# Router products in column tiles and modulation chunks spread over the q/k products, in a two-layer diffusion step on one core

## The reference, cut to what matters

```python
def grouped_moe(h, w_router, router_bias, w_gate, w_up, w_down):
    t = h.reshape(-1, D)                                    # 640 tokens, D = 1024
    scores = jax.nn.sigmoid((t @ w_router).astype(f32))     # 16 experts
    biased = scores + router_bias
    # best of 4 groups by the sum of its two best, then the best 2 experts in it
    ...
    gates = ...                                             # normalised scores of the two
    act = silu(t @ w_gate[e]) * (t @ w_up[e]) * gates
    return act @ w_down[e], summed over e

for layer in range(2):
    shift_a, scale_a, gate_a, shift_f, scale_f, gate_f = split(silu(cond) @ w_ada[layer] + b, 6)
    h = modulate(rmsnorm(x, norm_mix[layer]), shift_a, scale_a)
    out = mla(h) if layer == 0 else neighbourhood_attention(qkv(h))
    x = x + gate_a * (out @ w_o)
    h = modulate(rmsnorm(x, norm_ffn[layer]), shift_f, scale_f)
    x = x + gate_f * grouped_moe(h, ...)
```

## Time and profile before

| | |
|---|---|
| median of 3 runs | 1524.39 us (1524.38 to 1531.06) |
| the profiled execution | 1526.28 us, span 1524.5 us |
| PE busy | 1306.5 us, 86% of the span |
| DVE, ACT, POOL busy | 495.0, 357.3, 262.5 us |
| mean granted clock of TensorE | 0.936 of full speed |

### The profile page before, as it was taken

The page is one execution under the profiler, slowest core; times in us unless marked ns, Lnnn a source line. Parts: engine busy times, 40 slices in busy tenths (PEclk is TensorE's granted clock), DMA queues, the critical chain, the costliest instruction groups (busy, mean ns, idle before and its releaser), DMA issues.

```text
span 1524.5 us, 19501 instructions
## 1 busy us (share of the span) xinstructions
PE 1306.5 (86%) x7230; PEld 756.4 (50%) x7230; DVE 495.0 (32%) x1249; ACT 357.3 (23%) x843; POOL 262.5 (17%) x374
## 2 busy tenths in 40 slices
PE   3899899999999678999839989998999968999980
PEld 2565466666555434444324445556774543444430
DVE  2221344444345511112261000005663661111227
ACT  3221344444312101111132000005662210111112
POOL 6112201000100131111050111301110013111104
PEclk9999999999999689999959999999999968999995
DMA  7723112211532648898762464503204144889855
GB/s 271 278 91 110 56 57 78 91 57 57 197 142 84 235 132 331 325 343 338 280 257 75 166 209 166 180 0 98 64 22 157 42 179 145 332 328 351 326 225 206
DMA packets 48616, 269.87 MB, mean 177 GB/s; under 512 B 9709, under 2 KB 16269, under 8 KB 34829
## 3 DMA queue, kind: packets, MB, share of 16 engines
q1 hardware_dynamic: 22588, 192.87, 34.9%
q0 software_dynamic: 18176, 47.65, 8.7%
q10 hardware_dynamic: 7776, 28.32, 4.6%
HBM read 235.49 MB, written 31.74 MB: 175 GB/s over the span
## 4 chain that ended last, share of the span: by engine, by line
PE 65%; DMA 16%; DVE 7%; issue 5%; ACT 3%; POOL 1%; SPq 1%; ACTq 0%; POOLq 0%; DVEq 0%; PEldq 0%
PE PS L735 12%; DMA weights<-in_gu 11%; PE PS L948 9%; PE PS L1068 9%; PE PS L986 8%; PE PS L657 7%; PE PS L1003 5%; PE PS L854 4%; PE PS L669 3%; PE PS L885 2%; DVE big L1464 2%; DMA resid<-in_x 2%; PE PS L813 2%; DMA weights<-in_ada 1%; PE PS L895 1%
## 5 line engine op out<-in xcount | busy, mean ns | idle before, releaser
L986 PE MATMUL PS<-weights,big 128*128 128x512 f32 x544 | 249.2, 612 | 27.7 <-DMA weights<-in_gu 24.2
L986 PEld LDWEIGHTS PS<-weights,big 128*128 128x128 f32 x544 | 103.5, 195 | 152.4 <-issue 152.2
L657 PE MATMUL PS<-const,big 128*128 128x128 f32 (+2 forms) x643 | 99.6, 296 | 72.4 <-ACT big L1171 28.5
L948 PE MATMUL PS<-weights,ht 128*128 128x512 f32 x320 | 144.1, 606 | 1.7 <-DVE ht L1464 1.6
L657 PEld LDWEIGHTS PS<-const,big 128*128 128x128 f32 (+2 forms) x643 | 82.8, 151 | 121.0 <-issue 68.1
L1068 PE MATMUL PS<-ht,weights 128*128 128x128 f32 (+1 forms) x512 | 140.2, 434 | 1.6 <-PE PS L669 1.0
L735 PE MATMUL PS<-weights,ht 128*128 128x336 f32 (+1 forms) x320 | 122.0, 540 | 6.4 <-DVE ht L1555 2.4
L1003 PE MATMUL PS<-weights,big 128*128 128x512 f32 x272 | 124.8, 602 | 1.8 <-DVE big L1867 1.8
L1068 PEld LDWEIGHTS PS<-ht,weights 128*128 128x128 f32 x512 | 77.8, 191 | 64.4 <-issue 64.4
L1464 DVE TENSOR_TENSOR big<-big,PS 128x256 f32<-128x256 f32 x34 | 14.3, 421 | 267.0 <-ACT big L1370 257.6
L948 PEld LDWEIGHTS PS<-weights,ht 128*128 128x128 f32 x320 | 60.6, 194 | 73.1 <-issue 73.1
(11 more groups left out here) (204 smaller groups left out, 1611.8 us busy)
## 6 DMA issues: line engine op xcount, KB each, us to landing
weights<-in_gu SPq DMA_DIRECT2D x34, 2048.0 KB, 11.5
weights<-in_ada SPq DMA_DIRECT2D x24, 2048.0 KB, 8.3
weights<-in_down SPq DMA_DIRECT2D x34, 1024.0 KB, 5.8
yrows<-big ACTq DMA_DIRECT2D x34, 512.0 KB, 10.4
weights<-in_qkv SPq DMA_DIRECT2D x6, 2048.0 KB, 8.5
weights<-in_wo SPq DMA_DIRECT2D x4, 2048.0 KB, 8.7
rows<-modrows POOLq DMA_DIRECT2D x16, 512.0 KB, 10.4
rows<-toeplitz SPq DMA_DIRECT2D x48, 128.0 KB, 2.8
```

Of the source, the lines that this page charges most:

```text
L657: return pe.transpose(dst, src, const[0:n, C_ID:C_ID + n])
L948: ins = pe.matmul(bank(4 + j), OT[:, k, t * P:(t + 1) * P], w[j][:, k, :], start=(k == 0), stop=(k == KD - 1))
L986: ins = pe.matmul(bank(0), gatT[:, k, :], w[:, k, :], start=(k == 0), stop=(k == KD - 1))
```

## The change

There are two edits, and a few semaphores are merged to make room for two new ones.

The router's products change sides. The 16 columns of the router become the weights, and the 128 tokens of the tile stream past. The eight products of a tile go to four column tiles, two accumulating in each, so that PSUM bank 3 holds four partial sums, 16 experts by 128 tokens, at partitions 0, 32, 64 and 96. ScalarE copies this block of 128x128 to SBUF (`lgT`), and one product with the copy as weights and a 0/1 matrix (`C_SEL`, 128x16) as the moving side adds the four parts and turns them back to 128 tokens by 16 experts, where the sigmoid reads them. VectorE clears the two strips of bank 3 once a layer. In the order of work, `logit_parts` stands ahead of the modulation chunk, and `logits` behind `counts`.

The chunks 8 to 11 of layer 1 move from behind the products 0, 2, 5 and 7 to behind 3, 6, 9 and 12. The order of loads is not edited.

```diff
-NCONST = 1078
+C_SEL = 1078
+NCONST = 1094
...
+    c[:, C_SEL:C_SEL + E] = p[:, None] % 32 == np.arange(E)[None, :]
...
+        lgT = [big(7040 + i * P, P) for i in range(2)]
...
-        ADA_QK = (0, 2, 5, 7)
+        ADA_QK = (3, 6, 9, 12)
...
-                pool.wait_ge(ko_ca, 1)
-                pool.wait_ge(ko_cd, 1)
+                pool.wait_ge(kc_ta, 2)
+                pool.wait_ge(kc_td, 2)
...
-            def logits(l, t):
+            def logit_parts(l, t):
 
                 s = f"f{l}"
                 pe.wait_ge(n_ta, hcol(s, t + 1))
                 pe.wait_ge(n_td, hcol(s, t + 1))
                 if t == 0:
                     pe.wait_ge(s_par, 64)
-                else:
+                    pe.wait_ge(rr_m, (NT + 1) * l + 1)
+                at = 3 * 512 + t % 2 * P
+                for k in range(2):
+                    for g in range(4):
+                        n = 2 * g + k
+                        ins = pe.matmul(PS[32 * g:32 * g + E, at:at + P], wrt[:, n * E:(n + 1) * E], hT[:, n, t * P:(t + 1) * P],
+                                        start=(k == 0), stop=(k == 1))
+                ins.then_inc(rr_lt, 1)
+
+            def logits(l, t):
+
+                pe.wait_ge(rr_lc, NT * l + t + 1)
+                if t:
                     pe.wait_ge(rr_sg, NT * l + t)
-                for k in range(KD):
-                    ins = pe.matmul(bank(6, E, t * E), hT[:, k, t * P:(t + 1) * P], wrt[:, k * E:(k + 1) * E], start=(k == 0), stop=(k == KD - 1))
-                ins.then_inc(rr_lg, 1)
+                pe.matmul(bank(6, E, t * E), lgT[t % 2], const[:, C_SEL:C_SEL + E], start=True, stop=True).then_inc(rr_lg, 1)
 
             def counts(l, t):
 
-                pe.wait_ge(rr_m, NT * l + t + 1)
+                pe.wait_ge(rr_m, (NT + 1) * l + t + 2)
                 M = rt[:, MZ + t * E:MZ + (t + 1) * E]
...
+                    if t:
+                        logit_parts(l, t - 1)
                     if l == 0 and t < 4:
                         ada(1, t)
+                    if t >= 2:
+                        counts(l, t - 2)
                     if t:
                         logits(l, t - 1)
-                    if t >= 2:
-                        counts(l, t - 2)
                 pe.wait_ge(g_mm["wo"], 2 * NT * (l + 1))
                 release(name, 0, 0)
                 release(name, 0, 1)
 
                 x_transposes(s, NT - 1)
+                logit_parts(l, NT - 1)
+                counts(l, NT - 2)
                 logits(l, NT - 1)
-                counts(l, NT - 2)
                 counts(l, NT - 1)
...
+                def parts(t):
+
+                    act.wait_ge(rr_lt, NT * l + t + 1)
+                    act.activation(lgT[t % 2], bank(3, P, t % 2 * P), ACT.Copy).then_inc(rr_lc, 1)
...
                         store(t - 1)
                         columns(t - 1)
+                        parts(t - 1)
...
                 columns(NT - 1)
+                parts(NT - 1)
                 scores(NT - 1)
...
+                dve.memset(bank(3, 2 * P), 0.0).then_inc(rr_m, 1)
```

More of the change, by code:

```diff
@@ L277, in build @@
         qk_mm, qk_ea, qk_ed = sem("qkT_done"), sem("qkT_act"), sem("qkT_dve")
-        kc_in, kc_tr, kc_ta, kc_td = sem("natcache_in"), sem("kcT_transposed"), sem("kcT_act"), sem("kcT_dve")
-        ko_tr, ko_ca, ko_cd, ko_out = (sem(n) for n in ("kout_transposed", "kout_act", "kout_dve", "kout_stored"))
+        kc_in, kc_tr, kc_ta, kc_td = sem("natcache_in"), sem("kc_ko_transposed"), sem("kcT_kout_act"), sem("kcT_kout_dve")
+        ko_out = sem("kout_stored")
         vs_in = [sem(f"v_shifted{j}") for j in range(2)]
-        rr_lg, rr_sg, rr_m, rr_cnt, rr_pos, rr_sc, rr_tab, rr_hot, rr_info = (sem(n) for n in (
-            "logits", "scores", "choice", "ranks", "positions", "slots_scattered", "tile_table", "first_slots", "first_info"))
+        rr_lt, rr_lc, rr_lg, rr_sg, rr_m, rr_cnt, rr_pos, rr_sc, rr_tab, rr_hot, rr_info = (sem(n) for n in (
+            "logitsT_parts", "logitsT_copied", "logits", "scores", "choice", "ranks", "positions", "slots_scattered", "tile_table", "first_slots", "first_info"))
         e_gw, e_dw, e_inf, e_gt, e_gi, e_ys = ([[sem(f"moe{l}_{n}{i}") for i in range(2)] for l in range(DEPTH)] for n in (
@@ L1079, in _ @@
                         ins = transpose(bank(4, P, c * P), kT[:, c, 512:640])
-                    ins.then_inc(ko_tr, 1)
+                    ins.then_inc(kc_tr, 1)
             def nat_scores(w):
@@ L1132, in _ @@
             pe.wait_ge(qk_ed, 8)
-            pe.wait_ge(ko_ca, 1)
-            pe.wait_ge(ko_cd, 1)
+            pe.wait_ge(kc_ta, 2)
+            pe.wait_ge(kc_td, 2)
             pe.wait_ge(g_ea["vproj"], 5)
@@ L1429, in _ @@
                 if n == 8:
-                    act.wait_ge(ko_tr, 1)
-                    act.activation(kout[:, 0:512], bank(4), ACT.Copy).then_inc(ko_ca, 1)
+                    act.wait_ge(kc_tr, 2)
+                    act.activation(kout[:, 0:512], bank(4), ACT.Copy).then_inc(kc_ta, 1)
             warm(ACT.Exp)
@@ L1794, in f_stage @@
                 link(dve.reciprocal(sm[7], sm[6]))
-                dve.wait_ge(rr_m, NT * (l + 1))
+                dve.wait_ge(rr_m, (NT + 1) * (l + 1))
                 link(tt(pay2[:, :, 1:3], M[:, :, 0:2], sc[:, :, 0:2], ALU.mult))
@@ L1943, in _ @@
                 if n == 8:
-                    dve.wait_ge(ko_tr, 1)
-                    dve.tensor_copy(kout[:, 512:], bank(5)).then_inc(ko_cd, 1)
+                    dve.wait_ge(kc_tr, 2)
+                    dve.tensor_copy(kout[:, 512:], bank(5)).then_inc(kc_td, 1)
             for w in range(NW + 3):
```

## The result

The changed kernel took 1518.23 us, the median of 11 runs (1513.62 to 1523.38); the kernel before, run again beside it, 1526.98 (1522.82 to 1532.2, 11 runs). The ratio is 0.9943, 95% interval 0.9923 to 0.9962: 8.7 us faster, between 5.8 and 11.8. The forecast was 13.1 us faster, a time of 1511.3 us in a range of 1506.5 to 1518. The profiled execution took 1518.23 us with a span of 1516.5, 8.0 us less than that of before.

The account below looks back on a forecast made before the run. It took TensorE products to lead the chain that ended last, with expert weight transfers and ScalarE/VectorE work between. Terms -7.3 - 3.4 - 1.4 - 3.3 + 2.3 = -13.1 us took 1524.39 to 1511.3 us, range 1506.5 to 1518.

Parts of the forecast that it names:

- Part 1: Q and k products: moving the modulation chunks removes the wait for weights behind product 0, -7.3 us.
- Part 2: Both output projections: router products in column tiles take less TensorE time, -3.4 us in the first and -1.4 in the second.
- Part 3: First output projection, tiles 1 and 2: shorter small work keeps the clock up for the wide products, -3.3 us.
- Part 4: Last tile of each output projection: the 0/1 product waits behind the counts of tile 3, +1.14 us, twice: +2.3.
- The sum: Whole kernel: all terms together give -13.1 us, 1513.2 us for the profiled execution and 1511.3 for the median.
- Rival (a): First output projection: the clock still falls, depending on where a stretch starts; 3.3 us stay, 1514.6 us; chance 0.20.
- (b): Q and k products: the wait moves to product 12, its load landing 11.4 us late; 1522.7 us; chance 0.07.
- (c): Router products: the column tiles don't overlap, 4.5 us instead of 0.67 in six blocks; 1537.7 us; chance 0.03.
- (d): Q and k products: loads move along with the chunks and each is late again; 1518 to 1524 us; chance 0.03.

Follow-up runs that it names:

- tail_order: The changed kernel with the last tile's 0/1 product put ahead of the counts of tile 3; 1514.08 us, ratio 0.9903 to the kernel before.
- before_again: The kernel before, without any edit, run once more for a second profile; 1529.55 us, ratio 1.0009.
- the two steady kernels: The changed kernel and the kernel before, each with the additions; 1511.03 us and 1523.81 us.
- the additions: To both kernels: two extra products ahead of gate and up products waiting for weights; loop's first weight load waits for ten scatters (scatter wait). Changed 1511.03 us, before 1523.81.
- changed_again: The changed kernel, without any edit, run once more for a second profile; 1519.64 us, ratio 0.9933 to the kernel before.
- chunks_only: The kernel before with only the modulation chunks moved behind products 3, 6, 9 and 12; 1518.99 us, ratio 0.9929.
- changed_warm: The changed kernel with only the extra products ahead of gate and up products that wait for weights; 1512.72 us, ratio 0.9897 to the kernel before.
- router_only: The changed kernel with the modulation chunks put back behind products 0, 2, 5 and 7; 1524.98 us, ratio 0.9968 to the kernel before.

## Why the prediction was wrong, point by point

- **Part 1, the chunks: right.** -7.3 forecast, -7.5 in the q/k stage. No wait came at product 12. The room on GpSimd's queue was overrated by 6 us, at no cost here.
- **Part 2, the router products: right in its mechanism, low by 1.0 us.** The tiles start 0.45 us ahead of the chunk (0.42). Leaving them cost 0.18 where 0.33 was taken, so routing 0 is 7.2 us shorter up to the last tile (6.0 and the 1.14 lost there) where 3.4 + 3.3 were forecast. Routing 1 is 1.9 shorter (0.8 and 1.14) where it was 1.4: at tiles 1 and 2 the tiles with the way out of them took 0.57 us where the sum had 0.67 + 0.33, and going in, which the sum had at nothing, cost 0.10 at each of three places. The Trainium skill, TensorEngine Tiling (Array Packing), Key Properties, has a drain at each change of tiling. The trace agrees, with a price on both sides: 0.10 us going in and 0.18 coming out. The prediction read the missing gap at 439.36 as no cost on entering; together the two sides are still under the 0.33 that it took for one.
- **Part 3, the clock: right for the profiled execution, a chance beyond it.** No wide product behind the changed small work is cold in any of the profiles with that edit. But the kernel before doesn't pay for two every time: of five profiles with the old routing three have both (112.4) and two have one (110.73). Rival (a) named this mechanism for the kernel after; it is true of the kernel before.
- **Part 4, the last tile: right.** +1.14 forecast, +1.14 measured. Undoing it gave 1.65 us in each layer (106.39 to 104.74, 98.25 to 96.61), more than it had cost: in tail_order VectorE goes on 0.14 us behind the choice of tile 3 (1222.87 to 1223.01), where even the kernel before took 0.63.
- **The sum, and the range: this step failed.** In the three edited stages the change is worth 14.3 us in the first pair of profiles (13.0 with before_again as the kernel before), and 12.8 in the medians of the two steady kernels, for 13.1 forecast. The step that failed is the passage from the terms to the time: "1513.2 for it, and 1524.39 - 13.1 = 1511.3 for the median", with a range made of the terms' bounds alone. Of the 6.9 us between 1511.3 and the 1518.23 measured, 2.6 are the base and 4.3 the gain. The base was the median of three runs that spread 6.7 us, and it was low: in the later sets of 11 to 18 runs the kernel before had 1526.98 to 1529.55. From 1526.98 the same sum gives 1513.9. For the other 4.3 the sum has no term: it took the expert stages behind the edits as fixed, without a reason. They vary by 3.1 us each in two executions of one program, and by 4 to 5 over the seven profiles without the additions, by cold products of 1.7 us and by how soon a load follows the last scatter. With both taken out, the difference of the two kernels is 12.8.
- **What stays open.** The 8.7 us of the first comparison are less than 12.8, and the interval's end is 11.8. The second comparison, changed_again, had 0.9933 (0.9908 to 0.9957), which reaches 14.1. Whether without the additions the changed kernel meets more cold products on average isn't settled by seven profiles, but they lean that way: 4, 4, 4 and 2 in layer 0 with the router change, 2, 2 and 3 without it, and the one product above cold in four of four against one of three. The times lean the same way: the additions are worth 5.0 us to the kernel before (1528.81 to 1523.81) and, by the ratios to it, 7.6 to 9.2 us to the changed one (0.9933 and 0.9943 to 0.9883), on different chips. The share of chance in the missing 4.3 us is open.

Of the other rivals none came true: (b) the load at product 12 was there in time, (c) the tiles overlap (0.63 us for the sixteen instructions), (d) no chunk waits for its weights.

## What to carry to other kernels

Where a later stage waits in turn for weights and for a clock, a gain ahead of it can read as "given back" in a pair of profiles. Profile the unchanged kernel twice before explaining it, count from more than three runs, and take their spread into the range. In the last tile the product that needed only ScalarE's copy stood behind counts that waited for VectorE; putting it ahead of them gains 1.65 us a layer in tail_order. With the two additions and that order the kernel runs at 1508.4 us, 1.3% under the kernel before and faster than the changed one.

## What the runs showed of the hardware that was not expected

A TensorE that is done sooner can make the stage longer. In layer 1 the end of the first gate and up product sets when the next 2 MB load is issued, against ten scatters that are issued at their own pace. The eight profiles without the scatter wait, from the earliest load to the latest (us; a minus means that the load was issued first):

| profile | load behind the last scatter | the scatter took | scatter to gather of next rows | first to third gate and up product |
|---|---|---|---|---|
| chunks_only | -0.23 | 7.86 | 14.91 | 35.25 |
| changed | -0.08 | 8.38 | 15.41 | 35.71 |
| changed_warm | 0.22 | 7.84 | 14.83 | 33.80 |
| router_only | 0.35 | 8.15 | 15.10 | 34.01 |
| changed_again | 0.65 | 5.72 | 13.18 | 33.61 |
| tail_order | 0.91 | 2.90 | 12.89 | 31.76 |
| before | 1.20 | 2.12 | 12.88 | 31.98 |
| before_again | 1.29 | not in the chain | 12.73 | 32.20 |

It is not a matter of which is issued first: the scatter was as late with a load 0.35 us behind it as with one ahead. The two kernels stand on both sides of the table, chunks_only with the old routing at its top.

Sixteen instructions (eight products) with 16-column weights in four column tiles cost 0.45 us of TensorE ahead of a chunk in the same tiling, and 0.57 with the way out, where sixteen with 128-column weights cost 1.71. To that come the 0.10 us going in and 0.2 us for the 0/1 product.
